# Differential attention in a decoder layer: the scores run 104 instead of 72 tile columns ahead of the transposes

## The reference

```python
q = q.reshape(B, S, DIFF_HEADS, 2, DIFF_HEAD_DIM)      # two sets of 64-wide queries and keys a head
s = einsum('ibhqd,ibhkd->ibhqk', qblk, k) * scale + bias   # i = 0, 1
s = where(rel >= 0, s, -inf)                            # causal
p = softmax(s, axis=-1)
a = p[0] - lam * p[1]
o = einsum('bhqk,bhkd->bhqd', a, v)                     # v is 128 wide
```

## Time and profile before

| what | value |
|---|---|
| median of 3 runs | 2613.06 us (2609.3 to 2615.25) |
| the profiled execution | 2610.35 us, its span 2608.8 us |
| PE busy | 2335.7 us, 90% |
| DVE, ACT, POOL busy | 1377.8 (53%), 1216.8 (47%), 727.5 (28%) us |
| chain that ended last | DVE 1%, the rest under 1%: it names only the last steps of the experts |
| POOL L539, the sum of the two matrices | 128 instructions, 321.5 us |
| DVE L599, taking scores | 352 instructions, 277.4 us |
| PE L690, transposes | 1088 instructions, 280 ns each, 25.9 us idle ahead of them |

### The profile page before, as it was taken

One profiled execution on the slowest core, in us unless ns is written; L12 is line 12 of the kernel. 1 busy time (PEld: TensorE's weight loads), 2 busy tenths in 40 slices (PEclk: granted clock), 3 DMA queues, 4 the chain that ended last, 5 costly groups with the idle time before them and its releaser, 6 DMA issues. The chain is left out here.

```text
span 2608.8 us, 36721 instructions
## 1 busy us (share of the span) xinstructions
PE 2335.7 (90%) x11480; PEld 1871.8 (72%) x11480; DVE 1377.8 (53%) x2803; ACT 1216.8 (47%) x1640; POOL 727.5 (28%) x558
## 2 busy tenths in 40 slices
PE   4999999997999999999968999388999999999981
PEld 3888889995666666666647878376788888788760
DVE  6212121104667666766634666557664665666663
ACT  5111111113666666666643444256454554655653
POOL 0000000004666666676710101222222222222220
PEclk7999999998999999999979999599999999999995
DMA  5333334225324442442144332379888778888857
GB/s 186 134 112 128 112 128 120 63 63 144 90 76 106 104 98 76 110 111 61 45 136 169 129 121 105 135 257 361 285 301 270 251 248 287 290 296 301 306 177 274
DMA packets 207628, 441.45 MB, mean 169 GB/s; under 512 B 19081, under 2 KB 56113, under 8 KB 205490
## 3 DMA queue, kind: packets, MB, share of 16 engines
q1 hardware_dynamic: 188530, 379.46, 43.3%
q0 software_dynamic: 19008, 60.91, 9.2%
HBM read 338.55 MB, written 101.76 MB: 169 GB/s over the span
## 5 line engine op out<-in xcount | busy, mean ns | idle before, releaser
L1389 DVE TENSOR_TENSOR gu_lo<-gu_raw,gu_hi 128x2048 fp32r<-128x2048 f32 x128 | 293.2, 2291 | 130.0 <-issue 79.1
L599 DVE TENSOR_SCALAR_CACHE_REDUCE p_ring<-ps_s 128x512 f32<-128x512 f32 (+6 forms) x352 | 277.4, 792 | 153.6 <-PE ps_s L670 149.3
L539 POOL TENSOR_TENSOR p_ring<-p_ring 128x1152 f32<-128x1152 f32 (+15 forms) x128 | 321.5, 2512 | 10.7
L564 ACT ACTIVATE p_ring<-p_ring,shift 128x1152 f32<-128x1152 f32 (+15 forms) x256 | 305.9, 1197 | 26.3 <-DVE shift L615 26.3
L705 PE MATMUL ps_o<-aT,v_st 128*128 128x512 f32 (+3 forms) x640 | 292.0, 540 | 0.0
L553 ACT ACTIVATE aT<-ps_t 128x512 f32<-128x512 f32 (+1 forms) x320 | 168.7, 531 | 222.8 <-PE ps_t L690 221.9
L1331 ACT ACTIVATE gu_hi<-gu_raw 128x2048 fp32r (+1 forms) x128 | 237.9, 1915 | 29.2 <-PEq L756 15.8
L1463 PE MATMUL ps_g<-gu_hi,xT_lo 128*128 128x512 f32 x720 | 236.1, 409 | 7.5 <-DVE xT_lo L1404 7.5
L1463 PE MATMUL ps_g<-gu_hi,xT_hi 128*128 128x512 f32 x720 | 227.7, 397 | 0.0
L1463 PE MATMUL ps_g<-gu_lo,xT_hi 128*128 128x512 f32 x720 | 227.7, 397 | 0.0
L537 POOL TENSOR_SCALAR p_ring<-p_ring,coef 128x1152 f32<-128x1152 f32 (+15 forms) x128 | 150.5, 1176 | 231.2 <-DVE coef L628 228.8
(11 more groups left out here) (218 smaller groups left out, 4405.1 us busy)
## 6 DMA issues: line engine op xcount, KB each, us to landing
gu_raw<-in_moe_w_gate SPq DMA_DIRECT2D x128, 512.0 KB, 8.8
gu_raw<-in_moe_w_up SPq DMA_DIRECT2D x128, 512.0 KB, 10.0
d_raw<-in_moe_w_down SPq DMA_DIRECT2D x64, 1024.0 KB, 7.4
qk<-stage SPq DMA_DIRECT2D x64, 512.0 KB, 2.8
q_first<-qk SPq DMA_DIRECT2D x64, 256.0 KB, 5.1
q_second<-qk SPq DMA_DIRECT2D x64, 256.0 KB, 5.1
w_raw<-in_diff_w_in POOLq DMA_DIRECT2D x12, 1024.0 KB, 6.9
k<-qk SPq DMA_DIRECT2D x8, 1024.0 KB, 12.5
```

The lines of the kernel that those rows point to most:

```text
L539: pool.tensor_tensor(p0(r, 0, w), p0(r, 0, w), p1(r, 0, w), ALU.add).then_inc(mixed, 1)
L564: nc.scalar.activation(p, p, ACT.Exp, bias=shift[:, r % 8, m:m + 1], accum_out=sums[:, r % 8, m:m + 1]).then_inc(raised, 1)
L599: ins = nc.vector.tensor_scalar(p(r, k0, k0 + far), ps_s[:, c % 2, 0:far], SCALE, None, ALU.mult, ALU.max, accum_out=top[:, r % 4, m, col: ...
L1389: nc.vector.tensor_tensor(gu_lo[:, j * GC:(j + 1) * GC], raw(half, j), gu_hi[:, j * GC:(j + 1) * GC].bitcast(F32), ALU.subtract).then_inc( ...
```

## The change

The lead becomes 104 columns. It starts at the same 72, since `BEGIN` is still -18, and grows by one column a step over the first 32 steps, all of them in the first head. `p0_ring` grows by the same 32 columns, to 172; the room comes from `gap`, a tensor of 3072 that nothing used, and from `o_sb`, which moves behind `near_place`. `inv` gets 32 rows instead of 16, since a row now waits longer between its `weigh` and its `out`. `p1_ring`, the PSUM buffers, the number of instructions of each kind and their sizes stay.

```diff
-    LEAD = 72
-    P0, P1 = 70 * 256, 24 * 256
+    LEAD0, LEAD = 72, 104
+    P0, P1 = 86 * 256, 24 * 256
...
-    BEGIN, END = -LEAD // 4, NU + 8
+    BEGIN, END = -LEAD0 // 4, NU + 8
...
-        while c < NC and scored_cost < turned_cost + LEAD:
+        while c < NC and scored_cost < turned_cost + min(LEAD, LEAD0 + max(0, n)):
...
-        o_sb = sb("o_sb", [P, 2, 4, P])
-        sb("gap", [P, 3072])
         sb("q_first_place", [P, 2, 2, 512], F32R)
...
+        o_sb = sb("o_sb", [P, 2, 4, P])
...
-        inv = sb("inv", [P, 16, 2])
+        inv = sb("inv", [P, 32, 2])
...
-                nc.vector.reciprocal(inv[:, r % 16, :], sums[:, r % 8, :]).then_inc(inverted, 1)
+                nc.vector.reciprocal(inv[:, r % 32, :], sums[:, r % 8, :]).then_inc(inverted, 1)
...
-                r = 4 * g % 16
+                r = 4 * g % 32
```

More of the change, by code:

```diff
@@ L628, in weigh @@
                 nc.vector.scalar_tensor_tensor(out=coef[:, r % 8, :], in0=sums[:, r % 8, 0:1], scalar=neg_lam[:, 0:1],
-                                               in1=inv[:, r % 16, 1:2], op0=ALU.mult, op1=ALU.mult).then_inc(coefed, 1)
+                                               in1=inv[:, r % 32, 1:2], op0=ALU.mult, op1=ALU.mult).then_inc(coefed, 1)
             def out(g):
```

## The result

The change makes the kernel faster: 2573.36 us (median of 4 runs, 2569.86 to 2577.08) against 2614.15 (4 runs, 2609.3 to 2616.64), a ratio of 0.9846 with a 95% interval of 0.9826 to 0.9867. The prediction said 2571, and 41.9 us less; measured are 40.8. The profiled execution of the kernel after took 2577.08 us, its span 2575.5, 33.3 us less than the span before.

The account below looks back on a forecast made before the run. PE was taken to bound the attention, losing time to waits for POOL and DVE and a lowered clock. 25.9 + 14.9 + (19.1 - 10.5) - 3.5 - 4.0 = 41.9 us less gave 2571 us, 8-in-10 range 2553 to 2604.

Parts of the forecast that it names:

- The wait for POOL: PE's wait for POOL's sum at each head's first transpose of the 13-to-16-tile quad: gone in all eight, 25.9 us gained.
- The clock: PE's lower clock over 8 us behind the waits for POOL: 14.9 us gained whole, bounds 0 and 14.9.
- Work that only moves and the memory: 32 score columns moving from last head to first, and new addresses of `o_sb`, `gap`, `inv`: 0 us.
- 12 to 1, place C: Row of 12 tiles, then 1: POOL's sum holds DVE's coefficient, PE waits 7 x 1.5 = 10.5 us, before 19.1.
- 16 to 5, place B: Row of 16 tiles, then 5: coefficient slips ahead of POOL's sum, the next is held; 3.5 us lost over seven heads.
- The first head: Both transitions fall into it: PE waits 2.2 and 1.5 us, queries 0.3; together 4.0 us lost, ends 0 and 8.
- Queries: Query loads landing 6.7 us after issue against 7.55 us of cover: just hidden, 0, other end 1 us a head.
- B is caught: Rival: POOL's sum holds the 16-to-5 coefficient in seven heads, costing 32 us instead of 3.5; 2600 us; chance 0.17.
- The sum: Whole kernel: 25.9 + 14.9 + (19.1 - 10.5) - 3.5 - 4.0 = 41.9 us less, 2571 us.
- The slower rival: Coefficients held at B and C, each pulling PE's clock down: 12.1 us a head, 32 slower, 2645 us; chance 0.07.

Follow-up runs that it names:

- Experiment 2: The changed kernel with a lead of 80 columns instead of 104 (ring 148 columns); 2627.12 us, 1.0078 of the kernel before.
- experiment 3: The kernel before, with PE repeating the turn-back transposes 8 times in one quad a head, right before the wait for POOL; 2596.82 us against 2607.64, 0.9961.
- experiment 1: The changed kernel with the lead left at 72 columns, so only the memory changes remain; 2604.41 us against 2607.64 for the kernel before, 0.9988.
- experiment 9: The changed kernel without the ramp, lead 104 from the start; 2579.58 us against 2612.17 for the kernel before, 0.9876.
- experiment 7: The changed kernel with a lead of 96 columns instead of 104; 2569.47 us, 0.9842 of the kernel before.
- experiment 4: The changed kernel with the coefficient written with one tensor input and two scalars by pointer; 2551.48 us against 2607.64 for the kernel before, 0.9785.
- experiment 8: The changed kernel run once more, unedited; 2571.8 us, 0.9854 of the kernel before.
- experiment 5: The kernel before, lead 72, with the coefficient written with one tensor input and two scalars by pointer; 2593.11 us against 2611.66, 0.9936.

## Why the prediction was right

**The wait for POOL**, 25.9 us: gone in all eight heads, and nothing like it followed. Experiment 2 shows how near that was to failing: with a lead too short, the next thing late was not a sum but a maximum that DVE found too late. I had cleared "what is late next" by counting steps to the next quad only, which was enough for 104 columns and would have misled me at 80.

**The clock**, 14.9 us: right in kind, which experiment 3 shows, and above its interval in size: 10.8 us by medians (7.0 to 13.6). I had read the size from one execution, and it differs from one to the next: 18.2 us of dips in the profile before, 8.4 in that of experiment 1. In the pair of profiles of this result PE's busy time fell by 15.8 us. My "I see no loss behind them" of the waits for DVE was wrong in two heads, where 3.4 us were lost. The new waits, up to 1.88 us in the steady heads, did not bring the level down in the profile after; in experiment 9 one of 1.89 did. The wait of 2.40 us in the first head was followed by 0.79, in experiment 7 by 1.00. No run tells what decides.

**Work that only moves and the memory**, 0: experiment 1 shows it for the memory. No run measures the 32 moved columns alone; nothing in the result speaks against 0. For the transposes the page's group of them (busy us, mean ns, idle us before them) has 0.1 us of idle time left in the whole kernel:

```profile
L689 PE MATMUL ps_t<-ident,p_ring 128*128 128x128 f32 x1088 | 171.9, 273 | 0.1
```

**12 to 1, place C**: caught in six of seven, as I chose between close ends. I had the two coefficients 2.0 us apart and the boundary at 1.9; they lay 2.06 to 2.78 us apart where it was caught, and 1.84 where it was let through. I took 1.5 us of PE's time; the waits are 1.33, 1.49, 1.61, 1.61, 0, 1.19 and 1.50 us. The sum charged this place eight times (7 x 1.5, and 1.5 once more in the first head), but it occurs only seven times, the first of them in the first head: 1.5 us too many.

**16 to 5, place B**: let through in seven of eight heads, as expected, and caught once, for 1.88 us of PE's time where I had 2.7 for that case. The coefficient behind it was held 2.63 or 2.64 us in the other steady heads, where I had "up to 2.5", and cost PE at most 0.43 us, where I had 0.5. The rival "B is caught" happened in one head of the seven it needed, by a pause of DVE's that I had not looked for (experiments 4, 7 and 8).

**The first head**: 2.40 and 1.33 us of waits against my 2.2 and 1.5. The coefficient of the row of 5 was let through there, and the one behind it held 3.13 us (at 677.91). **Queries**: just hidden, no wait of PE's matmuls for them in the turning stretch.

**The sum.** For DVE I expected 10.5 + 3.5 + 4.0 = 18.0 us of waits to be left; it is 22.3, L601 and L598 together. C is 8.7 of them, B with the first head's 4.3, and 1.4 lie ahead of 652 us, in the attention's first steps. The remaining 7.9 us are waits of up to 0.47 us, behind 16 to 5 and ahead of the short rows' scores; of these I had foreseen only the 3.5 behind 16 to 5. So my gain at DVE of 19.1 - 18.0 = 1.1 us was in truth a loss of 2.4 (22.3 against 19.9), and the gain is all wait and clock. That the whole came out within 1.1 us of the forecast is partly luck: DVE was 3.5 us worse than I had it, and against the profile of experiment 1, with the same old order but fewer dips, the turning stretch after is only 30.7 us shorter instead of 40.0.

**The slower rival** needed 7.5 us a head of new losses with the clock's. There were 3.0 (22.3 us of waits and 1.7 of the one dip, over 8), so it was far off; but experiment 2 is its kind, a hold with 3.9 us of idle time behind it and the low clock (slower by 0.8%), at a place that I had not looked at.

## What to carry to other kernels

When a lead is lengthened to cover a wait, look at every small instruction that the new order puts beside a long one of POOL: what it holds up on DVE travels through ACT to PE, and a lead lengthened too little can be worse than one left alone. If such a small instruction of DVE has two tensor inputs and one of them is a single column, write it with that column as a scalar by pointer: 0.05 us more for each, and 0.6% less of the whole time here. Read what a pause of PE costs in two rows, the wait and the granted clock behind it; repeating harmless work in the pause tells the second apart. Take more than one profile for the second: the same order lost 18.2 us to it in one execution and 8.4 in another.

## What the runs showed of the hardware

- A coefficient that is there before POOL's scaling ends goes before POOL's sum, which starts 0.08 us after it: 7 of 8 heads at place B. In six of them it started 0.18 or 0.19 us before the end of the scaling and took its usual 0.22 us. In the first head it started 0.35 us before (676.03, the scaling until 676.38) and took 0.36: it was held by the scaling and let through between the two. At 920.51 it started 0.09 us behind the sum's start and was held 4.48 us. A difference of 0.35 us in its start thus made 4.3 us of hold.
- An instruction of DVE with one tensor input and two scalars by pointer, all from SBUF, took 272 to 277 ns in 256 of 256 cases (experiments 4 and 5), 124 of them beside work of POOL, while the form with two tensors takes 0.22 us when nothing holds it.
- Pauses of PE of 3.24 to 3.31 us were followed by a mean granted clock below 1.00 over the next 8 us (0.62 to 0.83) in 7 of 8 cases before, 5 of 8 in experiment 1 and 8 of 8 in experiment 5. After pauses of 1.74 to 2.40 us it fell in some executions (0.79 at 988.24 and 1165.36 before, at 682.42 after, at 930.44 in experiment 9) and not in others (926.13 after, 680.64 in experiment 7). Repeated transposes in the long pause kept it at 1.00.
